# Attention masks added by TensorE behind each head's scores; minima straight from PSUM

## What is computed

```python
# latent attention, one block of 128 queries
sc = jnp.einsum('bqhd,bkhd->bhqk', qi, k) * scale
sc = jnp.where(kpos[None, :] <= qpos[:, None], sc, -jnp.inf)
pr = jax.nn.softmax(sc, axis=-1)
# sliding window, the block itself and the one before
rel = WINDOW + i - j
valid = (rel >= 0) & (rel < WINDOW) & ((blk - 1) * WINDOW + j >= 0)
sc = jnp.where(valid, sc, -jnp.inf)
pr = jax.nn.softmax(jnp.concatenate([sc, sink], axis=-1), axis=-1)[..., :-1]
```

## Time and profile before

| | |
|---|---|
| three timed runs | 2460.81, 2468.52, 2468.61 us, median 2468.52 |
| profiled execution | 2461.51 us, its span 2459.8 us |
| TensorE matmul | 2336.3 us busy, 95% |
| TensorE weight load | 1886.6 us, 77% |
| VectorE | 1624.6 us, 66% |
| ScalarE | 1085.0 us, 44% |
| GpSimd | 1055.3 us, 43% |
| granted TensorE clock, mean | 0.976 |

### The profile page before, as it was taken

The page is one execution under the profiler, slowest core; times in us unless marked ns, Lnnn a source line. Parts: engine busy times, 40 slices in busy tenths (PEclk is TensorE's granted clock), DMA queues, the critical chain, the costliest instruction groups (busy, mean ns, idle before and its releaser), DMA issues. The chain is left out here.

```text
span 2459.8 us, 31600 instructions
## 1 busy us (share of the span) xinstructions
PE 2336.3 (95%) x11717; PEld 1886.6 (77%) x11717; DVE 1624.6 (66%) x2058; ACT 1085.0 (44%) x1790; POOL 1055.3 (43%) x675
## 2 busy tenths in 40 slices
PE   5999997999899999999999999889989999999997
PEld 5788765687788888888878887567867888888886
DVE  6974455636877667778887534564486676667885
ACT  4334535634444444444543453454334444444443
POOL 1212478423797777400011235123449877770000
PEclk7999998999999999999999999799999999999999
DMA  7651213043133333487556221002413333336763
GB/s 263 231 180 52 73 51 120 18 163 120 49 113 114 109 99 107 132 289 254 147 189 211 81 65 54 5 19 103 150 43 115 95 107 103 111 125 244 242 203 111
DMA packets 270823, 311.26 MB, mean 127 GB/s; under 512 B 34792, under 2 KB 189134, under 8 KB 269646
## 3 DMA queue, kind: packets, MB, share of 16 engines
q1 hardware_dynamic: 270382, 308.45, 38.9%
q10 hardware_dynamic: 288, 0.79, 0.1%
HBM read 246.98 MB, written 61.42 MB: 125 GB/s over the span
## 5 line engine op out<-in xcount | busy, mean ns | idle before, releaser
L954 POOL TENSOR_TENSOR wLo<-raw,wHi 128x1024 fp32r<-128x1024 f32 x66 | 161.2, 2443 | 414.3 <-ACT wHi L956 414.3
L1623 POOL TENSOR_TENSOR prodLo<-comb,prodHi 128x512 fp32r<-128x512 f32 x160 | 231.2, 1452 | 123.3 <-ACT prodHi L996 123.3
L1456 PE MATMUL bank<-tHi,prodHi 128*128 128x512 f32 x640 | 249.3, 390 | 1.1 <-POOL prodLo L1623 1.1
L1456 PE MATMUL bank<-tHi,prodLo 128*128 128x512 f32 x640 | 249.0, 389 | 0.0
L1456 PE MATMUL bank<-tLo,prodHi 128*128 128x512 f32 x640 | 249.0, 389 | 0.0
L1471 PE MATMUL bank<-gateHi,downHi 128*128 128x512 f32 x616 | 240.1, 390 | 0.0
L1471 PE MATMUL bank<-gateHi,downLo 128*128 128x512 f32 x616 | 239.7, 389 | 0.0
L1471 PE MATMUL bank<-gateLo,downHi 128*128 128x512 f32 x616 | 239.6, 389 | 0.0
L996 ACT ACTIVATE prodHi<-comb 128x512 fp32r<-128x512 f32 x160 | 100.9, 632 | 259.3 <-PE bank L1456 232.3
L2335 DVE SCALAR_TENSOR_TENSOR ub<-bank,ffp,ub 128x1023 f32<-128x1023 f32 x88 | 112.8, 1282 | 155.0 <-ACT ub L1882 153.4
L1456 PE MATMUL bank<-hHi,prodHi 128*128 128x512 f32 x480 | 189.0, 394 | 12.2 <-POOL prodLo L1623 12.2
(11 more groups left out here) (387 smaller groups left out, 5529.9 us busy)
## 6 DMA issues: line engine op xcount, KB each, us to landing
raw<-in_ffn_w_up_dram SPq DMA_DIRECT2D x88, 512.0 KB, 4.9
gateRaw<-gateOut SPq DMA_DIRECT2D x154, 256.0 KB, 4.2
adaE<-in_ada_w_dram SPq DMA_DIRECT2D x64, 512.0 KB, 5.9
gateOut<-gateSums SPq DMA_DIRECT2D x22, 1024.0 KB, 5.6
raw<-in_w_in_dram SPq DMA_DIRECT2D x34, 512.0 KB, 4.5
downRaw<-in_ffn_w_down_dram SPq DMA_DIRECT2D x66, 256.0 KB, 3.7
raw<-in_w_out_dram SPq DMA_DIRECT2D x28, 512.0 KB, 4.3
downCols<-in_ffn_w_down_dram SPq DMA_DIRECT2D x24, 512.0 KB, 3.7
```

Source lines behind the costliest of these rows:

```text
L954: eng.tensor_tensor(lo[:], raw[slot][:], fview(hi[:]), ALU.subtract).then_inc(s["split_lo"], 1)
L1456: last = mm(o, w[idx][:, c0], moving(idx, kp, hi), start=kp == 0 and q_ == 0, stop=kp == 3 and q_ == 2)
L1623: pool.tensor_tensor(sLoW[idx][:], product_source(js, idx), fview(sHiW[idx][:]), ALU.subtract).then_inc(s["us_lo"], 1)
```

## The change

The masks are added by TensorE. Identity and mask are rounded once per layer to the reduced fp32 type (`fp32r` in the profile) by two ScalarE operations, which stand behind the wait for the last pack of the input projection. Behind each head's scores comes one more product, identity times mask, that accumulates on the same columns: 256 columns in a sliding-window unit (128 in block 0), the last 128 columns in a latent unit. VectorE's two subtractions go, and it takes the minima from PSUM in both kinds of unit. The sink is no longer a column: its minimum with the scores is taken by an operation on 128x4 numbers, its distance to that by a second; ScalarE takes one exponential of 128x4 numbers behind the four heads; VectorE adds it to the sums before the reciprocal. The exponentials of a sliding-window unit go from PSUM to `swaProb`, and ScalarE instead of VectorE waits for the transposes that read that tile. The writes of the sink column go.

```diff
-    prs = [place(f"swaProb{i}", [P, SWA_H, 260], F32, R[13] + 4160 * i) for i in range(2)]
-    stat = {k: place(f"stat_{k}", [P, 3, 3, 4], F32, R[13] + 8320 + 192 * n) for n, k in enumerate("sm")}
+    prs = [place(f"swaProb{i}", [P, SWA_H, 256], F32, R[13] + 4096 * i) for i in range(2)]
+    stat = {k: place(f"stat_{k}", [P, 3, 5, 4], F32, R[13] + 8192 + 256 * n) for n, k in enumerate("sm")}
+    identR = place("identRounded", [P, P], F32R, R[13] + 8704)
+    maskR = place("maskRounded", [P, 2, P], F32R, R[13] + 9216)
...
 def scores(u):
-                        last = mm(o, sq[r, h % 2, i * BLK:(i + 1) * BLK], sk[r, lo:(i + 1) * BLK], start=True, stop=True)
+                        mm(o, sq[r, h % 2, i * BLK:(i + 1) * BLK], sk[r, lo:(i + 1) * BLK], start=True, stop=False)
+                        last = mm(bank[u % 2][:, h * 256 + (0 if i else BLK):(h + 1) * 256], identR[:], maskR[:, 0 if i else 1:2, :], start=False, stop=True)
...
-                            last = mm(bank[u % 2][:, q * HALF + a:q * HALF + b], qh[h][0:96, i * BLK:n], kh[h][0:96, a:b], start=True, stop=True)
+                            mm(bank[u % 2][:, q * HALF + a:q * HALF + b], qh[h][0:96, i * BLK:n], kh[h][0:96, a:b], start=True, stop=b < n)
+                        last = mm(bank[u % 2][:, q * HALF + i * BLK:q * HALF + n], identR[:], maskR[:, 1, :], start=False, stop=True)
...
 scalar engine, before the projections of the latent heads
+            act.wait_ge(s["pack_used"], nth("pack_used", N_WIN))
+            A(identR[:], ident[:], ACT.Copy)
+            A(maskR[:], band[:], ACT.Copy, scale=-1.0)
...
-            act.wait_ge(s["sw_m"], nth("sw_m", 1))
-            act.wait_ge(s["rope_dve"], nth("rope_dve", 3))
-            for i in range(2):
-                A(prs[i][:, :, 256], nsink[:], ACT.Copy).then_inc(s["sw_m"], 1)
...
 def exps(u):
+                    if i >= 2:
+                        act.wait_ge(s["un_t"], nth("un_t", LAST["s"][i - 2] + 1))
                     for h in range(SWA_H):
-                        a = prs[i % 2][:, h, 0 if i else BLK:257]
-                        last = A(a, a, ACT.Exp, bias=st_[:, 0, h:h + 1], scale=-1.0, accum_out=st_[:, 1, h:h + 1])
+                        lo = 0 if i else BLK
+                        A(prs[i % 2][:, h, lo:256], bank[u % 2][:, h * 256 + lo:(h + 1) * 256], ACT.Exp,
+                          bias=st_[:, 0, h:h + 1], scale=-1.0, accum_out=st_[:, 1, h:h + 1])
+                    last = A(st_[:, 4, :], st_[:, 3, :], ACT.Exp, scale=-1.0)
...
-                if kind == "s" and i + 2 < NB:
-                    act.wait_ge(s["un_e"], nth("un_e", u + 1))
-                    A(prs[i % 2][:, :, 256], nsink[:], ACT.Copy).then_inc(s["sw_m"], 1)
...
 def least(u):
-                    dve.wait_ge(s["sw_m"], nth("sw_m", 2 + i))
-                    if i >= 2:
-                        dve.wait_ge(s["un_t"], nth("un_t", LAST["s"][i - 2] + 1))
-                    lo = 0 if i else BLK
-                    s4 = bank[u % 2][:].rearrange("p (h k) -> p h k", h=4)[:, :, lo:256]
-                    link(dve.tensor_tensor(prs[i % 2][:, :, lo:256], s4, band[:].rearrange("p b k -> p (b k)")[:, lo:256].unsqueeze(1).to_broadcast([P, 4, 256 - lo]),
-                                           ALU.subtract))
-                    dve.tensor_reduce(st_[:, 0, :], prs[i % 2][:, :, lo:257], AX.X, ALU.min).then_inc(s["un_n"], 1)
+                    dve.wait_ge(s["sw_m"], nth("sw_m", 1))
+                    s4 = bank[u % 2][:].rearrange("p (h k) -> p h k", h=4)[:, :, 0 if i else BLK:256]
+                    link(dve.tensor_reduce(st_[:, 0, :], s4, AX.X, ALU.min))
+                    link(dve.tensor_tensor(st_[:, 0, :], st_[:, 0, :], nsink[:], ALU.min))
+                    dve.tensor_tensor(st_[:, 3, :], nsink[:], st_[:, 0, :], ALU.subtract).then_inc(s["un_n"], 1)
                 else:
                     n, k = (i + 1) * BLK, len(hs)
                     sc = bank[u % 2][:].rearrange("p (q n) -> p q n", q=k)
-                    diag = sc[:, :, i * BLK:n]
-                    link(dve.tensor_tensor(diag, diag, band[:, 1, :].unsqueeze(1).to_broadcast([P, k, P]), ALU.subtract))
                     dve.tensor_reduce(st_[:, 0, hs[0]:hs[0] + k], sc[:, :, 0:n], AX.X, ALU.min).then_inc(s["un_n"], 1)
 
 def inverse_of(kind, i):
+                if kind == "s":
+                    link(dve.tensor_tensor(st_[:, 1, :], st_[:, 1, :], st_[:, 4, :], ALU.add))
                 dve.reciprocal(st_[:, 2, :], st_[:, 1, :]).then_inc(s["sw_r" if kind == "s" else "ml_r"], 1)
```

More of the change, by code:

```diff
@@ L197 @@
     "dt_abs": 1, "dt_exp": 2, "dt_sum": 1, "dt_ln": 1, "dt_ready": 1, "mn_sq": 3, "mn_sum": 2, "mn_rstd": 3, "mn_dve":
-    3, "mp_full": 10, "mp_q": 12, "mp_kv": 10, "rope_dve": 3, "sw_vt": 1, "sw_vcopied": 1, "sw_m": 9, "k_rope": 48,
+    3, "mp_full": 10, "mp_q": 12, "mp_kv": 10, "rope_dve": 3, "sw_vt": 1, "sw_vcopied": 1, "sw_m": 1, "k_rope": 48,
     "un_s": 32, "un_n": 32, "un_e": 32, "un_t": 32, "un_ca": 32, "un_cd": 32, "un_o": 24, "sw_r": 8, "sw_b": 8, "sw_c":
```

## The result

Slower, by more than forecast: 2506.72 us (2497.23 to 2509.35, median of 4) against 2464.66 of the kernel before beside it; ratio 1.0165, 95% interval [1.0135, 1.0195]. The forecast was 2480, range to 2503: the direction was right, the size not. The profiled execution took 2509.35 us.

What follows compares the result with a forecast made beforehand. TensorE, busy for 95% of the span, was taken as the bound, with VectorE's and ScalarE's chain in sliding-window units. 20 (sliding-window units) + 0.4 (first units) + 3.5 + 0 (latent) - 6 (clock) = +18 us: 2480, range 2457 to 2503.

Steps and rivals of the forecast that it cites:

- Chain of a unit: Sliding-window units: TensorE waits for exponentials behind minima behind scores; removing the mask subtraction takes 1.25 us off VectorE's side.
- Side by side: Sliding-window scores: masks behind every head stop two heads running in the array's halves, 0.86 us more per unit.
- The rival of cheap masks: Sliding-window scores: pairs are one head's two records, so no overlap is lost; -4 us, 2457; chance 0.17.
- Mode changes: Sliding-window scores: 0.10 us per change between half and full array, seven more in a unit, 0.70 (bounds 0 and 0.8).
- How much of it is on the path: Sliding-window units after the first: of 2.0 us later scores, 1.1 to 2.0 count each; 10.0 us per layer.
- Small operations: VectorE on four numbers, sliding window: two at 0.20 us each, 0.40 in all; a third off the chain costs 0.
- Narrow products: TensorE's mask products: 0.11 us for 256 columns, 0.44 per sliding-window unit; 0.11 for 128 columns in latent units.
- The rival of the fp32 rate: TensorE's narrow rounded mask products run at fp32's rate, 25 us more: 2504; chance 0.12.
- the latent masks: Late latent units, one head: a 128-column mask product on TensorE, 32 x 0.11 = 3.5 us.
- Clock: Attention stages: shorter gaps return a fifth of 58 us at 1.2 GHz to 2.4, -6 us (bounds 0 and -20).
- first units: First sliding-window unit of each layer: scores 1.3 us later, but +0.2 us each in time, 0.4 for both.

Runs made afterwards that it cites:

- e5: Changed kernel with 14 of the 16 GpSimd steps beside stage 0 (layer 0's attention) cut to 8 of 1024 columns; medians differ by 4 us, stage 0 8.2 us shorter.
- e6: e2 with the sink copied by VectorE into a masked score column, without small operations with two SBUF operands; 2434.73 us, 1.15% faster than before.
- e3: Changed kernel without VectorE's three small operations and ScalarE's small exponential per sliding-window unit, so the sink has no part; 20.2 us less than the changed kernel.
- e8: Kernel before with all four heads of a sliding-window unit read from partitions 0 to 63 (wrong data), no masks on TensorE; ratio 1.0035 to before.
- e4: Changed kernel with sliding-window heads ordered 0, 2, both masks, 1, 3, both masks; 30.5 us below the changed kernel.
- e2: Changed kernel with the sliding-window masks written in front of the four heads, which accumulate on them; 37.5 us less than the changed kernel.
- e1: Kernel before with only the latent masks moved to TensorE, sliding-window units as they were; ratio 0.9998 to before.
- e9: Changed kernel with six idle 512-column products ahead of the transposes of each sliding-window unit but the first; 2508.43 us.
- e10: e1 with six idle 512-column products ahead of the transposes of each sliding-window unit but the first; 2450.87 us, ratio 0.9958 to before.

## Why the prediction was wrong in size

Unit by unit, from the start of one sliding-window unit's scores (or masks) to the next one's, us, blocks 0 to 1, 1 to 2 and so on:

```
layer 0  before  11.0  20.8  20.0  13.3  18.8  14.1  16.3
         after   13.7  29.2  22.6  16.0  22.0  21.0  19.0
         e5      11.4  22.9  26.6  16.1  19.9  19.4  19.0
         e6       8.0  17.0  18.7  12.8  16.8  15.9  16.4
layer 1  before  10.6  22.8  23.8  13.3  17.1  14.0  16.3
         after   11.1  22.9  26.6  16.1  19.9  19.6  18.7
         e6       8.0  17.0  18.7  12.6  15.0  13.6  16.4
```

*Chain of a unit, right.* Exponentials behind minima behind scores, TensorE waiting for them. Taking the subtraction off is worth about its 1.25 us: from the scores' end to the transposes, block 7 of layer 0 took 5.89 us before and 4.70 in e3.

*Side by side, right.* 0.86 forecast, 0.85 in e8. The rival of cheap masks, which hung on this, falls.

*Mode changes, wrong: one of the two failed steps.* "So 0.10 for each change; the masks add seven in a unit: 0.70 (bounds 0 and 0.8)". It is 0.20 each and 1.40 a unit (3.83 in after; the 2.20 of e4 fits the same value), outside the bounds. I had compared the time up to the first half-array record (0.92 against 0.82) and missed that the record behind it is late too (0.32 instead of 0.215 from first to second), and never looked for the way back. Two sequences that end in different places don't price a change; one that goes there and back does. The rule in the Trainium skill ("TensorEngine Tiling (Array Packing)", section Key Properties), that a change of tiling mode drains the engine, points the right way: e2, masks all on one side of the heads, is 37.5 us faster (with the heads side by side again, too). It gives no size.

*How much of it is on the path, too low.* I let 10.0 of each layer's 14 us count. Where nothing else interferes (blocks 3 to 4 and 6 to 7, both layers) a unit takes 2.4 to 2.8 us longer, which is the whole growth of the span, 2.69: there the growth goes by TensorE's side, and what the subtraction gave is lost. It is not the small operations: in e3 the same stretches take 15.8 and 18.6.

*Small operations, wrong: the other failed step, and the larger.* "0.20 each", the third "costs 0, and 0.2 if that cover were gone": some 6 us in all. They ran 23.1 us in after, 15.5 of it over the 0.16 that one takes alone, and cost 20 (e3). In stage 1, where GpSimd has little to do, two of the three have means of 0.16 and 0.15 (the third, 0.52, waited for GpSimd three times), and 0.40 holds in blocks 1 and 7 (from the scores' end to the transposes 4.25 in e3 and 4.74 in after; 4.70 and 5.11). The nearest row that I took, the reciprocal, has one operand; the nearest with two in SBUF was swaLo's (L2249), in the same trace, and I did not look at its spread: 0.40 to 2.40 us. The Trainium skill has it ("SBUF — State Buffer", section SBUF: two separate sides): a VectorE instruction with two SBUF inputs and a GpSimd instruction that reads SBUF share a port pair, which the one that starts first holds for its whole instruction. Every row above agrees, up to 2.35 us for four numbers. The price in time is greatest from block 1 to 2 of layer 0: 29.2 in after, 22.9 in e5. Not all of that stayed won, as the next stretch rose from 22.6 to 26.6. Both stretches of e5 are then those of layer 1 in after (22.9 and 26.6).

*Narrow products, right.* 256 columns have 0.11: e4's four fit it. The rival of the fp32 rate falls. 128 columns: 0.06, so 3.5 us for the latent masks was too much, and e1 found none.

*Clock, wrong in sign in the profiled execution.* I let the low clock shrink by a fifth of 58 us. It grew to 78.5, in stage 0 alone (20.5 to 44.4; stage 1 37.5 to 34.1). The reading behind the term, that the clock falls after idle time, does not carry it: TensorE's gaps over 0.3 us sum to 37.2 us in the stages before and to 33.5 after, so there was less idle time and more low clock. Two adjoining windows of after show what it costs, the second without any idle time, and two more, at the edges of a slow stretch in it, that TensorE had been busy for 15 us before the clock fell:

```profile
450.00:470.00 20.00, 17.02 (x135) 12.84 (x135) 8.18 (x16) 6.90 (x21) 8.64 (x4) 0.91 0.06 22
470.00:491.00 21.00, 21.00 (x120) 15.49 (x119) 10.52 (x17) 10.14 (x24) 7.34 (x4) 0.76 0.00 1
...
458.10:473.00 14.90, 14.90 (x108) 11.15 (x109) 4.11 (x9) 6.13 (x13) 3.19 (x3) 0.89 0.01 2
473.10:483.30 10.20, 10.20 (x48) 8.26 (x48) 6.56 (x9) 3.78 (x13) 5.80 (x3) 0.50 0.01 2
```

TensorE is busy for 21.00 of 21.00 us at 0.76, and the stretch from block 5 to 6 takes 21.0 us where it took 14.1. A busy engine at 1.2 GHz is a loss which the waits don't list. What made the clock fall there stays open.

A coarse sum with the measured sizes: spans 14 x 2.69 + 2 x 2.04 (first units, 0.72 to 2.76) = 41.8; subtractions 14 x -1.25 = -17.5; together 24, where e3 stands 22 above before. Small operations +20: 44. Measured are 42 in medians and 48 in the profiled executions. Of the 26 us between forecast and median, some 11 are thus the spans, if all of them count (14 x 0.70 from the mode changes and 2 x 0.74 from the first units, where 1.3 was forecast), and 14 the small operations. The parts are not additive, though (e2 and e6 show it), and the clock's share in after itself stays open, since e9 did not isolate it.

A slip in the rival of cheap masks: 1.14 less 0.85 is 0.29 and not 0.2, which makes its time 2459 instead of 2457 and changes no choice.

## What to carry to other kernels

Work that TensorE can take over for a few columns is cheap only in its own tiling mode: put it ahead of or behind all half-array products in a row, never between them, and keep products of different halves adjacent. Before adding a small VectorE operation on a path, count its operands in SBUF and look at what GpSimd runs at that time; one operand, or a value that rides along in a reduction that is there anyway, was worth 34 us here, together with the clock that rose with it. Read the granted clock of every stretch before and after: a busy engine can run at half speed, and less idle time alone did not bring the clock back (e3).

## What the runs showed of the hardware

- A change between half-array and full-array products costs 0.20 us at full clock (after and e4), half of it ahead of the first record and half between it and the next.
- TensorE's granted clock can fall to 1.2 GHz with no gap near (after, 473.1: busy for all of the 14.9 us before), and stages with less idle time can have more of it (18.0 and 61.4 us in e3, 22.1 and 3.4 in e6).
- Products on the two halves overlap also when both heads of one half are issued before those of the other, and still do so when they accumulate on a mask (1.14 us for eight records in before and e2, 1.99 when all are on one half, e8).
- A VectorE operation with two SBUF operands on 128x4 numbers takes 0.15 to 0.16 us alone and up to 2.35 us when a GpSimd operation is already running, with whose end it ends; a copy or reciprocal of that size stays at 0.17 to 0.18.
- Rounded products with 256 columns follow by 0.11 us, with 128 by about 0.06.
- Idle products in TensorE's waits can make a kernel faster (e10: 2466.17 to 2450.87), and can fail to (e9).
